# The output projection of latent attention: one native fp32 pass, or three rounded passes

## The reference, cut to what matters

```python
def _mla_branch(...):
    # 8 heads; q and k have 128 + 64 features, v has 128; causal in chunks of 64 tokens
    ...
    o = attention(q, k, v)                       # [tokens, 8 heads x 128]
    return (o * silu(m_z)) @ mla_w_o             # gated, then projected: 1024 -> 1024

merged = sigmoid(gate_a) * o_mla + sigmoid(gate_b) * o_rwkv + sigmoid(gate_c) * o_gla
```

## Time and profile before

| | us |
|---|---|
| median of 3 runs | 2036.11 (2035.39 to 2037.14) |
| profiled execution | 2040.9 |
| its span in the trace | 2039.1 |
| TensorE (PE) matmul busy | 1948.5 (96%) |
| VectorE (DVE) busy | 1313.0 (64%) |
| ScalarE (ACT) busy | 704.5 (35%) |
| GpSimd (POOL) busy | 76.9 (4%) |

### The profile page before, as it was taken

One profiled execution on the slowest core, in us unless ns is written; L12 is line 12 of the kernel. 1 busy time (PEld: TensorE's weight loads), 2 busy tenths in 40 slices (PEclk: granted clock), 3 DMA queues, 4 the chain that ended last, 5 costly groups with the idle time before them and its releaser, 6 DMA issues.

```text
span 2039.1 us, 41542 instructions
## 1 busy us (share of the span) xinstructions
PE 1948.5 (96%) x18039; PEld 1797.0 (88%) x18039; DVE 1313.0 (64%) x1710; ACT 704.5 (35%) x1011; POOL 76.9 (4%) x123
## 2 busy tenths in 40 slices
PE   7999999999899999999999999988999998999998
PEld 7988999998599999989887879987998887889987
DVE  8896487646658766864675349665764676429654
ACT  5562333334533332230423123243222234113143
POOL 2000000000400000010000000000002000000000
PEclk9999999999999998999999999998999999999999
DMA  8545478843347784645440236453663540135543
GB/s 221 139 135 165 137 245 262 261 136 114 99 144 256 250 240 110 165 125 146 123 115 5 74 104 174 118 147 101 169 163 103 146 134 14 44 104 157 144 121 108
DMA packets 473064, 291.41 MB, mean 143 GB/s; under 512 B 26680, under 2 KB 467485, under 8 KB 472777
## 3 DMA queue, kind: packets, MB, share of 16 engines
q1 hardware_dynamic: 466688, 262.20, 46.0%
q0 software_dynamic: 5312, 25.32, 3.4%
q10 hardware_dynamic: 904, 1.58, 0.4%
HBM read 288.02 MB, written 1.05 MB: 142 GB/s over the span
## 4 chain that ended last, share of the span: by engine, by line
PE 81%; DVE 12%; ACT 3%; issue 2%; DMA 1%; POOL 0%; DVEq 0%; ACTq 0%; SPq 0%
PE bank L702 40%; PE bank L1412 6%; PE bank L1414 5%; PE bank L1413 5%; PE bank L691 4%; PE bank L661 2%; DVE rounded L727 2%; PE bank L891 2%; PE bank L883 2%; PE bank L1615 1%; PE bank L1602 1%; PE bank L1057 1%; PE bank L784 1%; DMA whole<-in_ffn_w_down 1%; PE bank L1583 1%
## 5 line engine op out<-in xcount | busy, mean ns | idle before, releaser
L702 PE MATMUL bank<-rounded 128*128 128x256 f32 (+1 forms) x4440 | 545.5, 283 | 12.5 <-DVE rounded L727 10.0
L702 PEld LDWEIGHTS bank<-rounded 128*128 128x128 f32 (+1 forms) x4440 | 532.1, 189 | 21.0 <-DVE rounded L727 14.5
L727 DVE TENSOR_TENSOR rounded<-arena,rounded 128x1024 fp32r<-128x1024 f32 (+1 forms) x243 | 293.3, 1213 | 92.4 <-ACT rounded L716 78.5
L1412 PE MATMUL bank<-parts 128*128 128x256 f32 x1024 | 291.5, 285 | 4.2 <-DVE parts L2188 4.2
L1414 PE MATMUL bank<-parts 128*128 128x256 f32 x1024 | 290.5, 284 | 0.0
L1413 PE MATMUL bank<-parts 128*128 128x256 f32 x1024 | 290.4, 284 | 0.0
L702 PE MATMUL bank<-common,arena 128*128 128x256 f32 x1280 | 285.6, 380 | 0.1
L702 PEld LDWEIGHTS bank<-common,arena 128*128 128x128 f32 x1280 | 240.1, 189 | 40.1 <-issue 5.1
L767 ACT ACTIVATE arena<-bank 128x512 f32<-128x512 f32 x114 | 67.8, 598 | 437.8 <-PE bank L702 423.6
L1412 PEld LDWEIGHTS bank<-parts 128*128 128x128 f32 x1024 | 196.8, 192 | 5.3 <-DVE parts L2188 3.6
L1413 PEld LDWEIGHTS bank<-parts 128*128 128x128 f32 x1024 | 196.9, 192 | 0.1
(11 more groups left out here) (389 smaller groups left out, 2488.2 us busy)
## 6 DMA issues: line engine op xcount, KB each, us to landing
arena<-in_w_in SPq DMA_DIRECT2D x190, 512.0 KB, 3.8
whole<-in_ffn_w_gate_up SPq DMA_DIRECT2D x44, 1024.0 KB, 5.3
arena<-in_ada_w POOLq DMA_DIRECT2D x32, 768.0 KB, 6.4
whole<-in_ffn_w_down SPq DMA_DIRECT2D x16, 1408.0 KB, 7.3
arena<-in_rec_w_in SPq DMA_DIRECT2D x36, 512.0 KB, 3.8
arena<-in_att_w_qkv SPq DMA_DIRECT2D x24, 512.0 KB, 3.8
arena<-in_rec_w_out SPq DMA_DIRECT2D x16, 512.0 KB, 3.6
arena<-in_mla_w_o SPq DMA_DIRECT2D x16, 512.0 KB, 3.9
```

Of the source, the lines that this page charges most:

```text
L702: last = pe.matmul(psum[s][0:c, m % 2 * T:m % 2 * T + T], w[a][:, k, cols], x[b][:, k, :], start=(k, a, b) == (0, 0, 0), stop=k == job.kt ...
L727: dve.tensor_tensor(raw_view(job_of[u], u, UNIT_LOW), raw, high_view(job_of[u], u).bitcast(F32), ALU.subtract)\
L1412: pe.matmul(bank, w_hi, x_hi, start=start and k == 0, stop=False)
```

## The change

The projection `mo` becomes a split stream with high parts by ScalarE. Its activations, the gated heads, are divided into OM_HIGH and OM_LOW, two new buffers of 8 x 256 each. ScalarE rounds each head as soon as VectorE has gated it, and VectorE subtracts one head later. The pieces keep their places. ScalarE also makes the high parts of the projection's units 0 and 1 in steps 4 and 5 of the attention, and those of units 2 to 7 after it; VectorE makes the low parts of units 0 and 1 behind heads 2 and 3, and the rest between its evictions.

```diff
-                "mo": merge("mla_w_o_2", OM),
+                "mo": merge("mla_w_o_2", (OM_HIGH, OM_LOW), "scalar"),
...
+        def tile_pieces_pe(job, ks, ready):
+            s, rounds = job.at % 2, job.at // 2
+            for k in ks:
+                if k == 0:
+                    for i in range(2):
+                        pe.wait_ge(unit_low.sem, split_at[job.first + i] + 1)
+                    pe.wait_ge(taken[s].sem, rounds)
+                pe.wait_ge(ready.sem, ready.due(pe))
+                for i in range(2):
+                    w = high_view(job, job.first + i), raw_view(job, job.first + i, UNIT_LOW)
+                    for a, b in ((0, 0), (0, 1), (1, 0)):
+                        last = pe.matmul(psum[s][:, i * T:i * T + T], w[a][:, k, :], job.rhs[b][:, k, :],
+                                         start=(i, k, a, b) == (0, 0, 0, 0), stop=k == job.kt - 1 and a == 1, skip_group_check=True)
...
                 if i == 9:
-                    native_pieces_pe(j["mo"], range(4), heads_out)
+                    tile_pieces_pe(j["mo"], range(4), heads_out)
                 if i == 10:
-                    native_pieces_pe(j["mo"], range(4, 6), heads_out)
+                    tile_pieces_pe(j["mo"], range(4, 6), heads_out)
 
             attend_pe(8, score, lambda h, s: VM[:, s, h * P:h * P + P], (MPR, MPT), vbanks, meanwhile)
-            native_pieces_pe(j["mo"], range(6, 8), heads_out)
+            tile_pieces_pe(j["mo"], range(6, 8), heads_out)
...
+            def low_of_head(h):
+                dve.wait_ge(gated_high.sem, gated_high.due(dve))
+                dve.tensor_tensor(OM_LOW[:, h, :], OM[:, h, :], OM_HIGH[:, h, :].bitcast(F32), ALU.subtract)\
+                   .then_inc(heads_out.sem, 1)
+
             def take(h, bank, free):
                 dve.tensor_tensor(OM[:, h, :], bank, ZM[:, h, :], ALU.mult)\
                    .then_inc(free.sem, 1)
                 dve.wait_ge(free.sem, free.due(dve))
-                dve.nop().then_inc(heads_out.sem, 1)
+                dve.nop().then_inc(heads_gated.sem, 1)
+                if h:
+                    low_of_head(h - 1)
+                if h in (2, 3):
+                    split_v(j["mo"].first + h - 2)
 
             attend_v(8, 192 ** -0.5, const("chunks"), MSC, MMX, MSM, take)
+            low_of_head(7)
...
             def meanwhile(i):
                 if i == 2:
...
+                if i in (4, 5):
+                    high_act(j["mo"].first + i - 4)
+                if i >= 4:
+                    act.wait_ge(heads_gated.sem, heads_gated.due(act))
+                    act.activation(OM_HIGH[:, i - 4, :], OM[:, i - 4, :], ACT.Copy)\
+                       .then_inc(gated_high.sem, 1)
 
             attend_act(8, MSC, MPR, MPT, MMX, MSM, meanwhile)
+            high_act(j["mo"].through())
```

More of the change, by code:

```diff
@@ L352, in program @@
         ROTM = OM[:, 0:4]
+        OM_LOW, OM_HIGH = rounded(DK, T, at=second_base + 13056), rounded(DK, T, at=second_base + 19856)
         VM = buf(TT, D)
@@ L467, in program @@
         heads_out = sem("heads_out")
+        heads_gated, gated_high = sem("latent_heads_gated"), sem("latent_heads_high")
         guarded_squares = sem("guarded_squares")
@@ L1045, in program @@
         high_by_act = [[u for u in split_units if job_of[u].high == "scalar"]]
+        def tile_pieces_pe(job, ks, ready):
[11 more added lines that the diff above has]
+                                         start=(i, k, a, b) == (0, 0, 0, 0), stop=k == job.kt - 1 and a == 1, skip_group_check=True)
+                    if k == job.kt - 1:
+                        last.then_inc(unit_used.sem, 1)
         def native_pieces_pe(job, ks, ready):
@@ L3291, in mla_act @@
             take_units(act, j["ukn"], keep(KN, ACT.Copy), high_before(j["ukn"], 2))
-            take_units(act, j["ukv"], keep_tokens(VM), high_before(j["ukv"], 2), only=range(2))
+            take_units(act, j["ukv"], keep_tokens(VM), only=range(2))
             def meanwhile(i):
                 if i == 2:
-                    take_units(act, j["ukv"], keep_tokens(VM), high_before(j["ukv"], 2), only=range(2, 4))
+                    take_units(act, j["ukv"], keep_tokens(VM), only=range(2, 4))
+                if i in (4, 5):
[4 more added lines that the diff above has]
+                       .then_inc(gated_high.sem, 1)
             attend_act(8, MSC, MPR, MPT, MMX, MSM, meanwhile)
+            high_act(j["mo"].through())
         def rwkv_act(j, l):
```

## The result

The changed kernel takes 2045.2 us (median of 10 runs, 2040.7 to 2050.55); the kernel before took 2038.55 in the same comparison (10 runs, 2035.39 to 2042.66). The ratio is 1.003 with a 95% interval of 1.002 to 1.0041, so it is slower by some 6.1 us (3 thousandths of 2038.55). The forecast had 2.5 us. The profiled execution has a span of 2043.9 us, 4.8 more than before.

The account below looks back on a forecast made before the run. TensorE, busy for 96% of the span, was taken to bound the kernel. Per layer 0.85 us later plus 0.3 for restarts, +2.3 us in two layers, took 2036.11 to 2038.4, set at 2038.6; range 2036.3 to 2043.3 us.

Parts of the forecast that it names:

- The gain: Output projection, three rounded passes for one native: 4.5 us a layer, 3.4 from six whole units, 1.1 from two piecewise.
- the sum: The forecast's account of a layer's attention and projection: 4.5 us gained against 5.65 us of delay, 1.15 lost on balance.
- The delays: Added ScalarE and VectorE work in the attention makes TensorE 2.8 us late at the first piece, 4.2 at the third unit.
- in some 1.5 us (four halves in 2.99): POOL's scaling for head 6 in the attention: both halves at their old pace, so its transposes start at 921.8 us.
- B: Rival: in the attention, VectorE's two-SBUF-operand subtractions and POOL exclude each other, 1.7 us later per layer, 2042.0 us; chance 0.39.
- C: Rival: TensorE's clock falls in the stretch with more gaps, 2 us a layer, 2042.6 us; chance 0.05.
- The rest of the sum: The forecast's attention and projection terms without exclusion or clock fall: 1.15 us lost per layer on balance.
- +1.15: Forecast net loss per layer in us: next projection 0.85 later, plus 0.3 for restarts at five TensorE waits.

Follow-up runs that it names:

- e2: The changed kernel with the low parts of units 0 and 1 subtracting a bank instead of the high part in SBUF: 2039.24 us, ratio 1.0001.
- b1: The kernel before plus unused VectorE work behind heads 2 and 3, each time two 128x512 subtractions with one operand in a bank: 2048.54 us, one run.
- e1: The changed kernel with high and low parts of units 0 and 1 moved ahead of the attention's busy steps: 2033.66 us, ratio 0.998.
- e8: The changed kernel with three units split early, low parts from head 4 on directly behind gating, last pieces moved to match: 2028.59 us, ratio 0.9966.
- b2: The kernel before plus one unused 128x1024 VectorE subtraction behind each of heads 2 and 3, both operands in SBUF: 2046.81 us, one run.
- bw: The kernel before plus five unused 128x512 VectorE subtractions behind head 2 alone, one operand in a bank: 2046.88 us, one run.

## Why the prediction was wrong

**The gain: right, a little low.** From the third unit to the end of "k" the changed kernel needs 3.77 us less (3.4 in the sum). By the starts of the matmuls in the trace, the six units take 16.95 us (17.15 in the sum), and the first unit of "k" 2.88 us instead of 3.06.

**The delays: all there, in their places.** ScalarE's copy for head 3 starts at 915.54 us, 2.3 us late against the stage's start (2.9 in the sum). VectorE stands 0.66 us ahead of head 1's low part. TensorE waits 0.38 us in k=5, 1.09 in k=6, 0.56 ahead of the third unit; the sum had 0.4, 1.2 and 1. Without exclusion and clock (e2) the third unit is 3.74 us late, and the sum had 4.23.

**The step that failed** is the one that has POOL give the two halves "in some 1.5 us (four halves in 2.99)". They took 2.78 (918.76 to 921.54). The duration was read from a trace in which no VectorE instruction with two SBUF operands lay beside POOL, and was carried into one in which the change puts such an instruction there. The rival that said so (B) stood at 0.39 with 1.7 us a layer; alone the exclusion cost 1.00. B had POOL held for head 5 as well, and there it was not (1.50 us for both halves).

**What was taken apart came together.** The clock's fall (C, 0.05) was dismissed because gaps of 0.9 us had stood beside 1.00. But B makes the gap longer: 2.49 us. Behind it came the fall, 1.6 us a layer by e2, where a fall cost 1.7 between b1's two layers. B and C should have been one case.

**The rest of the sum was too dear.** Without both, the stage is level with before (0.0 and -0.3 us in e2), where +1.15 stood. The gain was 0.4 low. Independent instructions on ScalarE overlap (its high part of a head starts at 912.19, before the unit's ends at 912.29), and a head's high part takes 413 ns instead of the 498 of its nearest row. That the rest of the 1.2 us is these two was argued, not run. It was luck that this error made up for about half of the other: the exclusion and the clock took 2.6 us a layer for which the sum had nothing, and the total is only 1.3 off.

Together, per layer: 0.0 to -0.3 without both, exclusion +1.0, clock +1.6, which is the +2.4 measured. In absolute terms the median of 2045.2 us lies above the range, and the kernel before also stood 2.4 us higher in that comparison than in the three runs shown; by the ratio the change comes to 2042.2.

## What to carry to other kernels

A duration read from a trace holds beside the neighbours that it had there. Before moving a VectorE instruction with two SBUF operands, look at what POOL does in that stretch; if TensorE waits for POOL, put the instruction earlier or let one operand be a bank. A wait of TensorE that grows may be paid twice, as it was here behind seven of eight waits of 2.0 us and more, the second time through the clock of the work behind it. And work whose inputs are ready early belongs where its engine stands idle, not in the step that already sets the pace: the same instructions, placed earlier, turned 1.003 into 0.9966.

## What the runs showed of the hardware

The exclusion strikes one side only here, and the order of the starts goes with it. In these runs POOL's instruction was lengthened in every place where it began 0.01 to 0.07 us behind a VectorE subtraction with two SBUF operands: its 128x256 form to 2.20 and 1.95 us instead of 0.925 beside a unit-sized one, and to 1.15 beside a head's. VectorE's stayed as it was (1.22 and 1.23 us; 0.42 to 0.46 for a head's). The 2.20 us lie beside two subtractions in a row, from 919.27 and from 919.62 us. Where POOL's 128x256 half began first and alone, neither paid: in the changed kernel that of head 5 runs from 915.22 us and the subtractions begin at 915.67 and 916.01, and all keep their times. Layer 2 and both layers of e2 show the same, with 0.29 to 0.45 us between the two starts. Whether VectorE would be held by a POOL instruction that it follows more closely was not run.

One SBUF operand did no harm. Before the change, VectorE's minima (TENSOR_REDUCE, two of them in 0.74 us, from SBUF alone) lay beside POOL's halves of heads 1 and 2 and left the 128x256 ones at 0.93 us. The prediction had overlooked them when it called all that lay there tiny or a reader of banks.

The clock behind a wait of TensorE: 1.00 behind 1.10 (e1, e8) and 1.51 us (e2); 0.50 behind 2.02 with a wait of 1.17 one head ahead of it (b2), 2.49 and 2.53 (the changed kernel) and 4.38 us (bw); both outcomes behind 2.21 us in one execution (b1). Counted by layers, the clock fell in none of the 12 whose longest wait here was up to 1.51 us, and in 7 of the 8 with 2.02 us or more. What decides between them at 2.21 us stays open, and so does why it stayed low longer in one layer each of b2 and bw than in the other. One fall cost 1.6 to 1.7 us in five of the seven layers, 2.8 and 3.0 in those two.
